# Sparse attention in a two-layer decoder trunk: from step by step to groups of two key blocks, with another order of the query tiles

## The reference

```python
def selected_attention(q, k, v, pos, sel, slopes):      # per 128 queries, on the key blocks that sel names
    s = jnp.einsum('bghqd,bgqnld->bghqnl', qc, kg).astype(jnp.float32) * DK ** -0.5
    s = s - slopes[None, :, :, None, None, None] * dist[:, :, None]
    p = jax.nn.softmax(jnp.where(valid[:, :, None], s, NEG_INF) ...)
    return jnp.einsum('bghqnl,bgqnld->bghqd', p, vg)
def window_attention(q, k, v, pos, slopes):             # the same on the last 256 keys
...
    o = g[0] * o_cmp + g[1] * o_slc + g[2] * o_win
```

## Time and profile before

| | |
|---|---|
| median of three runs | 2252.74 us (2248.02 to 2253.5) |
| span of the profiled execution | 2245.4 us |
| sparse attention, first score to last value | 1341.56 to 1731.11 us of the span |
| PE, DVE, ACT, POOL busy in the whole span | 88%, 42%, 31%, 20% |

### The profile page before, as it was taken

One profiled execution on the slowest core, in us unless ns is written; L12 is line 12 of the kernel. 1 busy time (PEld: TensorE's weight loads), 2 busy tenths in 40 slices (PEclk: granted clock), 3 DMA queues, 4 the chain that ended last, 5 costly groups with the idle time before them and its releaser, 6 DMA issues. The chain is left out here.

```text
span 2245.4 us, 30273 instructions
## 1 busy us (share of the span) xinstructions
PE 1981.3 (88%) x11225; PEld 1262.1 (56%) x11225; DVE 947.7 (42%) x2302; ACT 698.9 (31%) x1761; POOL 456.3 (20%) x617
## 2 busy tenths in 40 slices
PE   6998859999969989859999768999999996999997
PEld 3444436655556756545655435666666555756664
DVE  3896874533252112114223486666664225211111
ACT  4013555531101111112122566667665110111111
POOL 0001003321022212110000255454544002122111
PEclk9999969999979999989999979999999997999999
DMA  5000010121387999863000200001001117799993
GB/s 216 0 0 0 0 47 20 39 88 66 153 362 285 383 348 377 314 210 70 1 0 1 78 1 11 11 11 48 20 11 34 77 72 316 256 379 364 353 340 119
DMA packets 80888, 307.77 MB, mean 137 GB/s; under 512 B 18352, under 2 KB 23495, under 8 KB 63846
## 3 DMA queue, kind: packets, MB, share of 16 engines
q1 hardware_dynamic: 66342, 272.23, 31.2%
q0 software_dynamic: 14400, 33.59, 5.9%
HBM read 276.75 MB, written 47.89 MB: 145 GB/s over the span
## 5 line engine op out<-in xcount | busy, mean ns | idle before, releaser
L1110 POOL TENSOR_SCALAR nsaatt_probs<-nsaatt_probs,nsaatt_inv,trunk_gates_or_logits 128x384 f32<-128x384 f32 (+7 forms) x256 | 185.6, 739 | 200.7 <-DVE nsaatt_inv L1137 200.7
L1123 DVE CUSTOM_DVE_ANT_0 nsaatt_probs<-nsaatt_scores,trunk_arena 128x384 f32<-128x384 f32 (+7 forms) x256 | 151.3, 629 | 86.3 <-PE nsaatt_scores L1029 85.7
L1834 DVE TENSOR_TENSOR experts_sig<-experts_gu_ps,experts_sig 128x256 f32<-128x256 f32 x50 | 21.2, 424 | 388.0 <-ACT experts_sig L1799 388.0
L1081 ACT ACTIVATE nsaatt_probs<-nsaatt_probs,nsaatt_bias 128x384 f32<-128x384 f32 (+7 forms) x256 | 169.0, 667 | 8.7 <-DVE nsaatt_bias L1132 8.6
L1039 PE MATMUL nsaatt_turn<-trunk_ident,nsaatt_probs 128*128 128x128 f32 x912 | 123.8, 279 | 23.4 <-POOL nsaatt_probs L1110 6.0
L1029 PE MATMUL nsaatt_scores<-layer_k_cols,trunk_x_rows 64*128 64x384 f32 (+3 forms) x640 | 128.9, 513 | 14.6 <-DVE nsaatt_top L1123 13.4
L1701 PEld LDWEIGHTS experts_gu_ps<-experts_x_cols,moew_w 128*128 128x128 f32 x1152 | 134.0, 197 | 12.1 <-issue 12.1
L1701 PE MATMUL experts_gu_ps<-experts_x_cols,moew_w 128*128 128x128 f32 x1152 | 136.7, 281 | 4.6 <-DVE experts_x_cols L1787 4.6
L1799 ACT ACTIVATE experts_sig<-experts_gu_ps 128x256 f32<-128x256 f32 x50 | 19.2, 383 | 381.0 <-PE experts_gu_ps L1701 243.6
L1039 PEld LDWEIGHTS nsaatt_turn<-trunk_ident,nsaatt_probs 128*128 128x128 f32 x912 | 97.3, 140 | 57.5 <-issue 37.6
L1713 PE MATMUL experts_gu_ps<-moew_w,experts_x_cols 128*64 128x512 f32 x256 | 97.0, 667 | 23.9 <-issue 23.9
(11 more groups left out here) (425 smaller groups left out, 3737.4 us busy)
## 6 DMA issues: line engine op xcount, KB each, us to landing
moew_w<-in_moe_w_gate_dram SPq DMA_DIRECT2D x34, 1024.0 KB, 12.4
moew_w<-in_moe_w_up_dram SPq DMA_DIRECT2D x34, 1024.0 KB, 18.2
moew_w<-in_moe_w_down_dram SPq DMA_DIRECT2D x34, 1024.0 KB, 25.6
trunk_arena<-in_moe_w_gate_dram SPq DMA_DIRECT2D x20, 1024.0 KB, 12.3
trunk_arena<-in_moe_w_up_dram SPq DMA_DIRECT2D x20, 1024.0 KB, 16.8
trunk_arena<-in_moe_w_down_dram SPq DMA_DIRECT2D x20, 1024.0 KB, 24.2
trunk_x_rows<-in_moe_w_gate_dram SPq DMA_DIRECT2D x10, 1024.0 KB, 16.3
trunk_x_rows<-in_moe_w_up_dram SPq DMA_DIRECT2D x10, 1024.0 KB, 22.3
```

The source lines that it names most:

```text
L1081: act.activation(part(s, r, h), part(s, r, h), ACT.Exp, bias=bias[:, b, i:i + 1], scale=steps[s]["scale"][h], accum_out=total[:, b, i:i + ...
L1110: pool.tensor_scalar(part(s, r, h), part(s, r, h), inv[:, s % BUFS, i:i + 1], 1.0 if gate is None else gate[h], ALU.mult, ALU.mult).then_i ...
L1123: dve.tensor_tensor_reduce(part(s, r, h), scores_of(s, r, h), br["mask"], 1.0, -3e38, ALU.add, ALU.max, top[:, s % BUFS, i:i + 1]).then_in ...
```

## The change

For the sparse attention (BR = 2) the order on PE, ACT and DVE is no longer by steps. All three walk over the groups n = 0 to 271. At each n PE does the values of group n - 5, the transposes of group n, and any score whose turn has come; a score stands a distance of 11 ahead of its own first transposes, its mask 10, its exponential 9, its inverse 4 or 5. The distance is counted in a weight of (blocks + 1) / 2.7 for each group. ACT now takes four groups of five to copy. The tiles come in the order 3 4 2 5 1 6 0 7, also in the list of `due`. Buffers, semaphores and the instructions themselves stay.

```diff
+SPARSE_ORDER = (3, 4, 2, 5, 1, 6, 0, 7)
+SCORE_LAG = 11
+MASK_LAG = 10
+EXP_LAG = 9
+INV_LAG = 4
+VALUE_LAG = 5
-    by_act = [n % 4 != 2 for n in range(len(flat))]
+    by_act = [n % (4 if BR == 1 else 5) != 2 for n in range(len(flat))]
+    opens = [n for n, g in enumerate(flat) if g[2] == 0]
+    weight = np.cumsum([0] + [(hi - lo + 1) / 2.7 for s, r, lo, hi in flat])
+    ENDS = range(-2 * SCORE_LAG, len(flat) + VALUE_LAG + 1)
+    def slot(u, lag):
+        at = weight[opens[u]] - lag
+        return int(np.floor(at)) if at < 0 else int(np.searchsorted(weight, at + 1e-9, side="right")) - 1
...
+                else:                                   # PE
+                    u = 0
+                    for n in ENDS:
+                        if 0 <= n - VALUE_LAG < len(flat):
+                            value(n - VALUE_LAG)
+                        if 0 <= n < len(flat):
                             turn(n)
+                        while u < S * BR and slot(u, SCORE_LAG) <= n:
+                            score(u // BR, u % BR)
+                            u += 1
...
+                else:                                   # ACT
+                    i = 0
+                    for n in ENDS:
+                        if 0 <= n < len(flat) and by_act[n]:
+                            copy_group(act, copy, n, copied_act)
+                        while i < S * SUB and slot(i // 2, EXP_LAG) + i % 2 <= n:
+                            exps(i // SUB, i % SUB // 2, i % 2)
+                            i += 1
...
+                else:                                   # DVE
+                    u = v = s = 0
+                    for n in ENDS:
+                        while v < S * BR and slot(v, INV_LAG + v % BR) <= n:
+                            inverse(v // BR, v % BR)
+                            v += 1
+                        if s < S and first[s + 1] - 1 + VALUE_LAG <= n:
+                            add(s)
+                            s += 1
+                        while u < S * BR and slot(u, MASK_LAG) <= n:
+                            mask(u // BR, 2 * (u % BR))
+                            mask(u // BR, 2 * (u % BR) + 1)
+                            biased(u // BR, u % BR)
+                            u += 1
+                        if 0 <= n < len(flat) and not by_act[n]:
+                            copy_group(dve, dve.tensor_copy, n, copied_dve)
...
-        for t in TILE_ORDER:
+        for t in SPARSE_ORDER:
```

More of the change, by code:

```diff
@@ L1055, in value @@
                     last.then_inc(valued, 1)
[L1057 to L1072 removed]
+                if BR == 1:
+                    for s in range(AHEAD):
+                        score(s, 0)
+                    for n in range(first[1]):
+                        turn(n)
+                    for s in range(S):
+                        if s + AHEAD < S:
+                            score(s + AHEAD, 0)
+                        for n in range(first[s], first[s + 1]):
+                            value(n)
+                        if s + 1 < S:
+                            for n in range(first[s + 1], first[s + 2]):
+                                turn(n)
+                else:
[4 more added lines that the diff above has]
+                        if 0 <= n < len(flat):
                             turn(n)
+                        while u < S * BR and slot(u, SCORE_LAG) <= n:
+                            score(u // BR, u % BR)
+                            u += 1
             @block.scalar
@@ L1150, in copies @@
                             copy_group(dve, dve.tensor_copy, n, copied_dve)
-                for s in range(AHEAD):
-                    for i in range(SUB):
-                        mask(s, i)
-                    for r in range(BR):
-                        biased(s, r)
-                    if s:
-                        for r in range(BR):
-                            inverse(s - 1, r)
-                copies(0)
-                for s in range(S):
-                    ahead = s + AHEAD < S
-                    if ahead:
-                        mask(s + AHEAD, 0)
-                        mask(s + AHEAD, 1)
-                        if BR > 1 and not wide(s + AHEAD):
-                            mask(s + AHEAD, 2)
-                            biased(s + AHEAD, 0)
-                            mask(s + AHEAD, 3)
-                    add(s)
-                    if ahead and wide(s + AHEAD):
-                        biased(s + AHEAD, 0)
-                        mask(s + AHEAD, 2)
-                        mask(s + AHEAD, 3)
-                    if s + AHEAD - 1 < S:
-                        for r in range(BR):
-                            inverse(s + AHEAD - 1, r)
-                    if ahead:
-                        biased(s + AHEAD, LAST)
-                    if s + 1 < S:
-                        copies(s + 1)
@@ new lines, in _ @@
+                if BR == 1:
+                    for s in range(AHEAD):
+                        mask(s, 0)
+                        mask(s, 1)
+                        biased(s, 0)
+                        if s:
+                            inverse(s - 1, 0)
+                    copies(0)
+                    for s in range(S):
+                        ahead = s + AHEAD < S
+                        if ahead:
+                            mask(s + AHEAD, 0)
+                            mask(s + AHEAD, 1)
+                        add(s)
+                        if s + AHEAD - 1 < S:
+                            inverse(s + AHEAD - 1, 0)
+                        if ahead:
+                            biased(s + AHEAD, 0)
+                        if s + 1 < S:
+                            copies(s + 1)
+                else:
[5 more added lines that the diff above has]
+                        if s < S and first[s + 1] - 1 + VALUE_LAG <= n:
+                            add(s)
+                            s += 1
[6 more added lines that the diff above has]
+                            copy_group(dve, dve.tensor_copy, n, copied_dve)
@@ L2763, in nsa_attention @@
     early = [t for ts in CHOSEN_EARLY.values() for t in ts]
-    due = {i: (0, t) for i, t in enumerate(TILE_ORDER) if t not in early}
+    due = {i: (0, t) for i, t in enumerate(SPARSE_ORDER) if t not in early}
     spread = (PER_GROUP_PAIRS - 1) * TILES // TILES
-    due.update({TILES + spread * i: (1, t) for i, t in enumerate(TILE_ORDER)})
+    due.update({TILES + spread * i: (1, t) for i, t in enumerate(SPARSE_ORDER)})
     order = sorted(due)
```

45 lines of the change are left out of this document (15 added, 30 removed).

## The result

The changed kernel takes 2272.35 us (median of 4 runs, 2270.36 to 2276.2) against 2252.5 for the kernel before (4 runs beside it, 2248.02 to 2253.5): ratio 1.0102, 95% interval 1.0085 to 1.012. It is slower by 1%. The two medians differ by 19.9 us, the ratio stands for 23 (the interval for 19 to 27). Forecast were 2275, in a range of 2262 to 2292. The profiled execution has a span of 2270.8 us, 25.4 more than before.

A forecast was written before the change was run, and what follows sets the result against it. PE was taken to bound the kernel. Visits +66.4, waits -42.8, remaining or new waits +5, later scores +1.3 and start -7.3 summed to +22.6 on 2252.7, so 2275.3 us, range 2262 to 2292.

The forecast's parts named there:

- A visit costs 0.15 us, and so visits cost +66.4 us: PE, steady part: each switch to turns or values costs 0.15 us, to scores 0.21; more visits add 66.4 us.
- rivals 2 and 3: PE visits: alternating runs of 4 pay no 0.15, 2209 us (chance 0.07); or about 0.10 us each, 2252 (chance 0.06).
- 0.21 for scores: PE, steady part: cost in us of each visit to scores, 24 more such visits adding 5.0 us.
- one load of 107 ns for a switch: PE switches: alternative estimate exposing one 128-column weight load each, 46 us in place of 66, sum 2255.
- Waits go, 42.8 us, and 5 stay: PE, steady part: nearly all 42.8 us of waiting goes; 5 us stays or is new, on additions and masks.
- rival 1: Step borders: values' single bank waits for its addition, 0.5 us at each of 64, 32 us not 5; 2302, chance 0.09.
- 0.2 us short: PE behind tiles 3 and 2: work falls some 0.2 us short of covering the addition, 3 us in all.
- The start, -7.3 us: First score to first turn: 11.0 us against 18.3, so -7.3 us (from -5 to -9).
- Scores that come later, +1.3: Steady part: scores done in the start fall from 54 blocks to 42, adding 1.3 us later.
- Copies, nothing: ACT and DVE: 14 more groups copied on ACT, some 8 us, covered by PE's own time.
- The sum: Whole kernel: +66.4 - 42.8 + 5 + 1.3 - 7.3 = +22.6 us, giving 2275.3; chance 0.78.

The follow-up runs named there:

- shape_128: Changed kernel with value matmuls loading 128 columns of weights instead of 64, so turns and values have one array form (timing only): 2337.3 us, ratio 1.0399.
- b3_spread_scores: As a3_cut_three, but two scores needing the same banks are never in one visit, the second going to the next run: 2240.07 us, ratio 0.9957.
- b3_addition_between: As b3_spread_scores, with DVE's addition of a step put between the masks of the two heads instead of behind both: 2228.42 us, ratio 0.9911.
- r1_alone: Changed kernel's runs of one group, but masks ahead of the addition on DVE and lags score 13, inverse 5: 2293.3 us, ratio 1.0191.
- e2_before_new_order: Kernel before with nothing but the new order of tiles 3 4 2 5 1 6 0 7: 2254.3 us, ratio 1.0022.
- e3_after_old_copies: Changed kernel with three of four copies by ScalarE, as before the change: 2274.5 us, ratio 1.0112.
- a3_cut_three: Changed kernel with turns and values in runs of at most three groups, ending at step borders, values two runs behind: 2244.9 us, ratio 0.9982.
- r2_pairs: As r1_alone, with values and turns in fixed runs of two groups: 2338.3 us, ratio 1.0391.
- a6_whole_step: Changed kernel with turns and values in runs of a whole step (up to six groups), values one run behind: 2344.2 us, ratio 1.0421.
- r3_triples: As r1_alone, with values and turns in fixed runs of three groups: 2338.4 us, ratio 1.0398.
- r4_fours: As r1_alone, with values and turns in fixed runs of four groups: 2367.4 us, ratio 1.0517.

## Why the prediction held, step by step

- **A visit costs 0.15 us, and so visits cost +66.4 us.** Right. 103.7 - 37.2 = 66.5 us. It was the step on which the sign hung, and rivals 2 and 3 said that a short visit or a turn straight behind a value pays less. 155 steps from turn to value have a median of 0.202 us and 267 from value to turn one of 0.203, and visits of 2 and of 4 alike pay 0.15. The prediction's 0.21 for scores is 0.206.
- **What the price is paid for.** The Trainium skill, TensorEngine Tiling, Key Properties, names a drain of TensorE at a change of tiling mode. shape_128 agrees that it hangs on the mode: without the change of form the 0.15 us is gone. That it is a drain is not shown. The prediction's estimate from the Trainium skill, TensorE: Matmul & The Clock Gate, section LDWEIGHTS, of one load of 107 ns for a switch, with 2255 as its sum, is not borne out by 2272. It also took 128 columns for every load; values load 64, 53 ns by the same formula, which would put the estimate at 2244, further off.
- **Waits go, 42.8 us, and 5 stay.** Right: 43.5 became 7.4, so -36.1 where -37.8 was said. It is right in detail too: before the first values behind tiles 3 and 2 PE comes 0.19 us late, 16 times, 3.0 us in all and each time 0.145 us behind the end of the addition, which no row of waits shows. But that only few stay rests on where the addition stands on DVE. The clean pair is b3_spread_scores with 19.0 us of waits for it and b3_addition_between with none; r1_alone, with masks ahead of it and other lags, has 14.2. The prediction gave rival 1 a chance for that same reason, DVE in the middle of a mask. What it called "0.2 us short" is an edge: in the kernels that have masks ahead of the addition the same wait is 12 to 80 us, so part of how close the forecast came is that this kernel stands on the good side of it.
- **The start, -7.3 us.** Mis-sized by 1.1: 18.3 became 12.1, -6.2. The prediction summed the scores and masks of three steps in place of four. In e2_before_new_order the fourth step alone takes 5.9 us, and the order of tiles without the order by groups shortens nothing (19.1).
- **Scores that come later, +1.3.** The pure work grows from 290.3 to 291.6 us. Right.
- **Copies, nothing.** Right, by e3_after_old_copies.
- **The sum.** 66.5 - 36.1 + 1.3 - 6.2 = +25.5 us; the spans differ by 25.4, the runs by 19.9 (medians) to 23 (ratio), and +22.6 was forecast. The terms that missed, 1.7 on the waits and 1.1 on the start, both leave the kernel slower than said.

One thing stays open: the first score of the phase stands between 1341.2 us (a3_cut_three) and 1351.0 (r2_pairs) in the traces, though nothing ahead of it was changed. The spans of single executions hold up to 10 us of this, and the account above, which begins at the first score, leaves it out.

## What to carry to other kernels

When matmuls of different array forms take turns on TensorE, count the changes of form and price each from starts in the trace; busy rows hide it. A finer order that removes waits pays only where what it adds in switches is less: of the orders tried here the best was between, runs of up to three groups that end where the accumulator changes hands. With a single accumulator bank, look early at what stands ahead of its addition in VectorE's order: taking one mask from there gave 11.7 us, and moving copies from one engine to the other gave nothing.

## What the runs showed of the hardware that was not expected

- Each f32 matmul of scores or values leaves two records. With half of the array (64 rows or 64 columns) the two start 7 ns apart, and the value matmul takes 0.109 us in all, no more than a transpose with its single record. With 128 columns the two records stand 0.112 us apart and the matmul takes 0.224. Half the columns thus took half the time, which is worth 105 us here; that the two records are two passes which run side by side in the array's halves fits this, but no run shows it by itself.
- The price of a change of form lies in two places: the first matmul of the new form starts 0.093 us late (0.202 for 0.109), and the second is late again, a transpose by 0.056 (0.165 for 0.109) and a value matmul by 0.051 (0.160). Together, with the 7 ns between the two records of a value matmul, these are the 0.15.
- At a change of form the weight load of the first matmul starts with it (at most 0.003 us ahead), where inside a visit to turns or values it starts 0.107 or 0.108 ahead.
- A wait of 2.86 us on PE in a6_whole_step is followed by work at nearly half speed (8 transposes in 1.92 us, granted clock 0.57), so this wait cost more than it lasted. In the four kernels with the most waits (117 to 169 us: r2_pairs, r3_triples, r4_fours, a6_whole_step) the granted clock of the steady part is 0.93 to 0.96, in the changed kernel 1.00.
